# Differential attention in a two-layer hybrid encoder: the shift of the second softmax map per half, three of four transpose copies on ScalarE, all scaling on GpSimd

## The reference

```python
def block(args):                       # one block of 128 queries
    qb, bi = args
    qpos = bi * BLOCK + jnp.arange(BLOCK, dtype=jnp.int32)
    bias = table[:, t5_bucket(kpos[None, :] - qpos[:, None])]
    sc = jnp.einsum('bqhmd,bkhmd->bmhqk', qb, k).astype(jnp.float32) * scale + bias[None, None]
    p = jax.nn.softmax(sc, axis=-1)
    a = p[:, 0] - lam * p[:, 1]
    return jnp.einsum('bhqk,bkhd->bqhd', a.astype(v.dtype), v)
```

## Time and profile before

| | us |
|---|---|
| median of 3 runs | 4045.36 (4042.28 to 4050.85) |
| the profiled execution | 4044.97 |
| its span in the profile | 4043.2 |
| `diff_attention` of the first layer, first matmul to last output | 1184.88 to 1693.16 |

### The profile page before, as it was taken

One profiled execution on the slowest core, in us unless ns is written; L12 is line 12 of the kernel. 1 busy time (PEld: TensorE's weight loads), 2 busy tenths in 40 slices (PEclk: granted clock), 3 DMA queues, 4 the chain that ended last, 5 costly groups with the idle time before them and its releaser, 6 DMA issues. The chain is left out here.

```text
span 4043.2 us, 51539 instructions
## 1 busy us (share of the span) xinstructions
PE 3793.2 (94%) x19002; PEld 2624.1 (65%) x19002; DVE 2236.1 (55%) x3973; ACT 1658.7 (41%) x2886; POOL 2286.1 (57%) x1381
## 2 busy tenths in 40 slices
PE   8999999999989999889989999999999899998898
PEld 8789774555546666557777897755555466665577
DVE  3003125555569999875531030255556699998755
ACT  3102103333348888760031021033333488887610
POOL 1221325877768888744512213267777688886455
PEclk9999999999999999999989999999999999999999
DMA  5433445233420222245354334422233202223353
GB/s 176 126 132 118 145 134 123 62 82 71 91 59 1 57 57 58 57 112 190 130 174 130 128 120 140 144 68 55 66 73 77 59 1 57 57 58 72 109 177 135
DMA packets 180864, 392.43 MB, mean 97 GB/s; under 512 B 18014, under 2 KB 100168, under 8 KB 168968
## 3 DMA queue, kind: packets, MB, share of 16 engines
q1 hardware_dynamic: 179752, 387.75, 34.3%
q10 hardware_dynamic: 864, 1.41, 0.2%
HBM read 255.93 MB, written 135.67 MB: 97 GB/s over the span
## 5 line engine op out<-in xcount | busy, mean ns | idle before, releaser
L1297 POOL TENSOR_TENSOR mla_sum_pool<-mla_sum_pool,mla_probs 128x1024 f32<-128x1024 f32 (+1 forms) x336 | 777.8, 2315 | 209.0 <-ACT mla_probs L1258 184.2
L1315 DVE TENSOR_REDUCE carry_row_max<-psum 128x1 f32<-128x512 f32 x688 | 474.2, 689 | 416.1 <-PE psum L1130 411.2
L1258 ACT ACTIVATE mla_probs<-psum 128x1024 f32<-128x1024 f32 x384 | 373.3, 1021 | 694.4 <-PE psum L1167 689.7
L1690 DVE TENSOR_REDUCE diff_row_max<-psum 128x1 f32<-128x1024 f32 x512 | 613.4, 1217 | 49.6 <-PE psum L1534 38.9
L1613 ACT ACTIVATE diff_probs<-psum,diff_shift 128x1024 f32<-128x1024 f32 x512 | 566.1, 1111 | 178.0 <-DVE diff_shift L1697 171.8
L1560 PE MATMUL psum<-ident,diff_probs 128*128 128x128 f32 x2048 | 328.1, 284 | 93.0 <-DVE diff_turned L1724 80.9
L638 PE MATMUL psum<-in_x_hi,in_w_hi 128*128 128x512 f32 x1024 | 409.4, 400 | 2.7 <-ACT in_mla_val L745 2.7
L638 PE MATMUL psum<-in_x_hi,in_w_lo 128*128 128x512 f32 x1024 | 405.5, 396 | 0.0
L638 PE MATMUL psum<-carry_firsts,in_w_hi 128*128 128x512 f32 x1024 | 404.5, 395 | 0.0
L1560 PEld LDWEIGHTS psum<-ident,diff_probs 128*128 128x128 f32 x2048 | 215.9, 141 | 265.0 <-issue 254.3
L1671 POOL TENSOR_TENSOR diff_probs<-diff_probs 128x1024 f32<-128x1024 f32 x128 | 305.8, 2389 | 141.6 <-ACT diff_probs L1621 141.3
(11 more groups left out here) (213 smaller groups left out, 7363.7 us busy)
## 6 DMA issues: line engine op xcount, KB each, us to landing
in_w_raw<-in_w_in SPq DMA_DIRECT2D x64, 512.0 KB, 3.9
split_d<-in_out SPq DMA_DIRECT2D x64, 512.0 KB, 2.7
raw_d<-in_out SPq DMA_DIRECT2D x32, 512.0 KB, 2.7
mq_d<-in_out SPq DMA_DIRECT2D x48, 256.0 KB, 3.6
mk_d<-in_out SPq DMA_DIRECT2D x48, 256.0 KB, 4.0
carry_firsts<-split_d SPq DMA_DIRECT2D x48, 256.0 KB, 8.1
carry_weights<-split_d SPq DMA_DIRECT2D x48, 256.0 KB, 7.7
carry_weights<-split_d SPq DMA_DIRECT2D x16, 768.0 KB, 18.1
```

The costliest lines, as they stand in the source:

```text
L1258: nc.scalar.activation(probs[:, s % RING, :].rearrange("p (a n) -> p a n", n=CH), psum[:, S0 + 2 * (s % 2):S0 + 2 * (s % 2) + 2, :], ACT.E ...
L1297: nc.gpsimd.tensor_tensor(acc, start, probs[:, s % RING, mine], ALU.add).then_inc(pool_added, 1)
L1315: nc.vector.tensor_reduce(row_max[:, u % 2, qb, n:n + 1], psum[:, sweep_bank(g), :], AX.X, ALU.max).then_inc(maxed, 1)
L1690: nc.vector.tensor_reduce(row_max[:, n % 2, m, half:half + 1], banks(n, m, half), AX.XY, ALU.max).then_inc(maxed, 1)
```

## The change

1. Scores come scaled. The queries of the differential heads are multiplied by 1/sqrt(32) as the input projection copies them out of PSUM (ACT's copy gets a scale, DVE's subtraction becomes a multiply and subtract), and the bias constants are no longer divided by it. The exponentials lose their scale.
2. Map 1 gets a shift for each half, `part_shift`, written by the maximum itself (a negated reduction). `exp` of a half of map 1 waits for that half's maximum alone. `to_shift` still makes the common shift of the map; ACT computes two correction factors `part` = exp(shift - part_shift) a unit, and DVE multiplies the two sums of map 1 by them before it adds up (the new instruction with semaphore `weighed`).
3. POOL does all scaling: two multiplications of 1024 columns, each by ratio and by the half's `part`; ACT's `scale` is gone.
4. ACT takes the transpose batches 0, 1 and 2, DVE takes batch 3. The lists of PE, ACT and DVE are reordered, so that there is one batch of transposes between two pieces of scores.

```diff
-            return (act_copied if c % 2 else dve_copied), 2 * n + c // 2 + 1
+            return (act_copied, 3 * n + c + 1) if c < 3 else (dve_copied, n + 1)
...
                         scores(n, 0, 0)
-                    turns(n - LAG - 1, 3)
+                    turns(n - LAG - 1, 1)
                     if on:
                         scores(n, 0, 1)
                     products(n, 0)
+                    turns(n - LAG - 1, 2)
+                    if on:
+                        scores(n, 1, 0)
+                    turns(n - LAG - 1, 3)
+                    products(n, 1)
                     turns(n - LAG, 0)
                     if on:
-                        scores(n, 1, 0)
-                    turns(n - LAG, 1)
-                    if on:
                         scores(n, 1, 1)
-                    products(n, 1)
-                    turns(n - LAG, 2)
...
+                def parts(n):
+                    act.wait_ge(shifted, 2 * n + 2)
+                    nc.scalar.activation(part[:, n % DEEP1, :], part_shift[:, n % 2, :], ACT.Exp,
+                                         bias=shift[:, n % 2, 1:2], scale=-1.0).then_inc(parted, 1)
...
                     if on:
-                        exp(n, 0)
-                    if n == UNITS:
-                        scale(n - 1)
-                    copy(n - LAG, 1)
-                    if 1 <= n < UNITS:
-                        scale(n - 1)
+                        exp(n, 0, 0)
+                        exp(n, 0, 1)
                     if n % 2:
                         odd_half((n - 5) // 2)
+                    copy(n - LAG, 0)
                     if on:
-                        exp(n, 1)
+                        exp(n, 1, 0)
+                    copy(n - LAG, 1)
+                    if on:
+                        exp(n, 1, 1)
+                        parts(n)
+                    copy(n - LAG, 2)
...
+                    for k, half in enumerate((0, 1) if n < LATE else (1,)):
+                        at = slice(half * HALF, (half + 1) * HALF)
+                        second = probs1[:, n % DEEP1, at]
+                        nc.gpsimd.tensor_scalar(second, second, ratio[:, n % 2:n % 2 + 1],
+                                                part[:, n % DEEP1, half:half + 1], ALU.mult, ALU.mult
+                                                ).then_inc(times_ratio, 1)
+                        pool.wait_ge(times_ratio, done + k + 1)
+                        nc.gpsimd.tensor_tensor(probs[:, n % DEEP, at], probs[:, n % DEEP, at], second, ALU.add
+                                                ).then_inc(mixed, 1)
...
                     dve.wait_ge(exped, 4 * (n + 1))
+                    dve.wait_ge(parted, n + 1)
+                    nc.vector.tensor_tensor(row_sum[:, n % 2, 1, :], row_sum[:, n % 2, 1, :], part[:, n % DEEP1, :],
+                                            ALU.mult).then_inc(weighed, 1)
+                    dve.wait_ge(weighed, n + 1)
                     nc.vector.tensor_reduce(totals[:, :, qb, h], row_sum[:, n % 2, :, :], AX.X, ALU.add
                                             ).then_inc(summed, 1)
...
                 for n in range(UNITS + DRAIN + 2):
                     on = n < UNITS
-                    copy(n - LAG - 1, 2)
                     if on:
                         maximum(n, 0, 0)
                         maximum(n, 0, 1)
                         to_shift(n, 0)
                     if n == UNITS:
                         mix(n - 2)
-                        ratios(n - 1)
-                        copy(n - LAG, 0)
+                    ratios(n - 1)
+                    if n == UNITS:
                         mix(n - 1)
-                    else:
-                        copy(n - LAG, 0)
-                        ratios(n - 1)
+                    copy(n - LAG - 1, 3)
                     if on:
                         maximum(n, 1, 0)
+                    if n % 2:
+                        output((n - 5) // 2)
+                    if on:
                         maximum(n, 1, 1)
                         to_shift(n, 1)
```

More of the change, by code:

```diff
@@ L369, in tile_banks, with tile_scale @@
             return psum[:, tile_slot(g):tile_slot(g) + 2, :].rearrange("p a n -> p (a n)")
+        def tile_scale(t):
+            return DIFF_SCALE if T_DQ <= t < T_DK else 1.0
         def use_freed(u):
@@ L833, in _ @@
                         else:
-                            nc.scalar.activation(out[:, s, :].bitcast(F32R), tile_banks(g), ACT.Copy).then_inc(tile_out, 1)
+                            nc.scalar.activation(out[:, s, :].bitcast(F32R), tile_banks(g), ACT.Copy, scale=tile_scale(t)
+                                                 ).then_inc(tile_out, 1)
             @block.vector
@@ L1428, in diff_attention @@
         dots = sb("dots", [P, 4])
-        row_max = sb("row_max", [P, 2, 2, 2])
+        row_max = sb("row_max", [P, 2, 2])
+        part_shift = sb("part_shift", [P, 2, 2])
         shift = sb("shift", [P, 2, 2])
+        part = sb("part", [P, DEEP1, 2])
+        late = sb("late", [P, UNITS - LATE])
         row_sum = sb("row_sum", [P, 2, 2, 2])
@@ L1602, in _, with exp @@
             def _(act):
-                def exp(n, m):
-                    act.wait_ge(shifted, 2 * n + m + 1)
-                    if m == 0 and n >= DEEP:
-                        act.wait_ge(turn_done, 4 * (n - DEEP + 1))
-                    if m == 1 and n >= DEEP1:
-                        act.wait_ge(mixed, 2 * (n - DEEP1 + 1))
+                def exp(n, m, half):
+                    if m == 0:
+                        act.wait_ge(shifted, 2 * n + 1)
+                        bias = shift[:, n % 2, 0:1]
+                        if n >= DEEP:
+                            act.wait_ge(turn_done, 4 * (n - DEEP + 1))
+                    else:
+                        act.wait_ge(maxed, 4 * n + 2 + half + 1)
+                        bias = part_shift[:, n % 2, half:half + 1]
+                        if n >= DEEP1:
+                            act.wait_ge(mixed, 2 * (n - DEEP1 + 1))
@@ L1609, in exp @@
                     dst = probs[:, n % DEEP, :] if m == 0 else probs1[:, n % DEEP1, :]
-                    if m == 0 and n >= 2:
+                    if n >= 2:
                         act.wait_ge(summed, n - 1)
-                    for half in range(2):
-                        nc.scalar.activation(dst[:, half * HALF:(half + 1) * HALF].rearrange("p (a n) -> p a n", n=CH),
-                                             banks(n, m, half), ACT.Exp, bias=shift[:, n % 2, m:m + 1], scale=DIFF_SCALE,
-                                             accum_out=row_sum[:, n % 2, m, half:half + 1]).then_inc(exped, 1)
@@ L1617, in scale @@
-                def scale(n):
-                    act.wait_ge(ratio_ready, n + 1)
-                    at = 0 if n < LATE else HALF
-                    first = probs1[:, n % DEEP1, at:at + CH]
-                    nc.scalar.activation(first, first, ACT.Copy, scale=ratio[:, n % 2:n % 2 + 1]).then_inc(act_scaled, 1)
+                    nc.scalar.activation(dst[:, half * HALF:(half + 1) * HALF].rearrange("p (a n) -> p a n", n=CH),
+                                         banks(n, m, half), ACT.Exp, bias=bias,
+                                         accum_out=row_sum[:, n % 2, m, half:half + 1]).then_inc(exped, 1)
@@ L1730, in mix @@
                     dve.wait_ge(ratio_ready, n + 1)
+                    factor = late[:, n - LATE:n - LATE + 1]
+                    nc.vector.tensor_scalar(factor, part[:, n % DEEP1, 0:1], ratio[:, n % 2:n % 2 + 1], None, ALU.mult
+                                            ).then_inc(late_ready, 1)
+                    dve.wait_ge(late_ready, n - LATE + 1)
                     nc.vector.scalar_tensor_tensor(probs[:, n % DEEP, 0:HALF], probs1[:, n % DEEP1, 0:HALF],
-                                                   ratio[:, n % 2:n % 2 + 1], probs[:, n % DEEP, 0:HALF],
+                                                   factor, probs[:, n % DEEP, 0:HALF],
                                                    ALU.mult, ALU.add).then_inc(dve_mixed, 1)
@@ L2468, in constants @@
     kb, qb = np.arange(NB)[:, None], np.arange(NB)[None, :]
-    far = f32(1.0 / DIFF_SCALE)
-    left, right = (kb <= qb - 2) * far, (kb >= qb + 2) * far
+    left, right = kb <= qb - 2, kb >= qb + 2
     lo_rows = (np.arange(2 * NB) >= NB).astype(f32)
```

56 lines of the change are left out of this document (27 added, 29 removed).

## The result

| | before | with the change |
|---|---|---|
| median, us | 4047.28 (4042.28 to 4050.85, 4 runs) | 4081.89 (4078.99 to 4083.55, 4 runs) |
| span of the profiled execution | 4043.2 | 4081.4 |
| ratio of the medians | | 1.0086, interval 1.0068 to 1.0103 |

The changed kernel is slower by 0.9%; 4,085 was forecast. As a difference, 40.6 us were forecast; the two profiled spans differ by 38.2 and the medians by 34.6, since one more run of the kernel before has moved its median from 4045.36 to 4047.28.

What follows compares the result with a forecast made beforehand. It took the single transpose bank and DVE's copy as the bound before (7.746 us a unit), a POOL and DVE ring after (8.07): 20.1 us a layer, +40.6 on 4044.97, so 4,085 us, range 4,060 to 4,104.

Steps and rivals of the forecast that it cites:

- The held instruction: DVE's new two-input multiplication of the sums waits for POOL's second addition to end: 0.8 to 1.8 us for 0.15.
- Rival 1: DVE's small multiplication of the sums is not held by POOL; 3,990 us, faster; chance 0.11.
- The pace: Distance from ratio to ratio, set by POOL and DVE: 8.07 us a unit, for 7.746 before.
- the second pointer operand of POOL's multiplication: POOL multiplying by ratio and part instead of ratio and a constant: 0.06 us each, bounds 0 and 0.08.
- Uniform over all units: The 8.07 us between ratios holds in every unit, whatever the query block.
- The ring: Ratio, POOL's multiplications and additions, held DVE instruction, next ratio: 7.95 us, 8.07 with the second pointers.
- The drain: After the last ratio of a layer, changed copies and POOL widths balance: 0, bounded by 2 us either way.
- Changes 1, 2 and 4 on other engines: Scaled scores cost zero; the new shifts, copies and order leave PE, DVE and ACT at 7.3 us a unit or less.
- PE's longer waits: Sign in the new trace: PE waits for more than before, spread over several places; no size given.
- The forecast for a kernel without the hold: Without DVE waiting for POOL, PE's ring and POOL's work set about 7.3 us a unit: 3,990 us.
- The ring of PE: PE's transposes, scores, bands and products with waits for copies: 7.27 us with the band in half 1, 6.82 in half 0.
- Rival 3: POOL's multiplication with two factors costs up to an addition's 2.37 us: pace 10.4, 4,375 us; chance 0.03.

Runs made afterwards that it cites:

- e1: Changed kernel with DVE's two-input multiplication of map 1's sums replaced by two one-input multiplications by pointer; 4012.60 us, ratio 0.9923 to the kernel before.
- e10: Changed kernel with DVE making one factor per half, no two-input multiplication of the sums, POOL multiplying by one pointer and 1.0; 4011.88 us, ratio 0.9921.
- e11: e10 with DVE's copy of transpose batch 3 put ahead of its last mixing in the drain; 4008.13 us, ratio 0.9912 to the kernel before.
- e8: e1 with POOL's second pointer replaced by 1.0, the halves' correction left out of the mixing; 4009.06 us in one run.
- e6: Changed kernel with DVE making one factor per half and POOL multiplying by one pointer with no second operation; 4389.74 us.

## Why the prediction was right, and where its steps were not

**The held instruction: right, in mechanism, place and size.** Forecast was 0.8 to 1.8 us, ending with POOL's second addition; it shows 1.25 and ends within 0.02 us of it. The Trainium skill (SBUF — State Buffer, on who interferes with whom), read literally, said so: what starts first keeps the ports for its whole length. The traces agree for both kinds of POOL instruction of 1024 columns, and e1 shows that a pointer form is free of it (204 ns beside a busy POOL). Rival 1 is out.

For very small POOL instructions the page's rule and the traces differ, and the measurement decides. Behind the earlier trace rows stand 32 such overlaps, not one: each of the 32 multiplications starts 0.07 to 0.15 us after a POOL power (operation `pow`) of 128 x 2, with 0.55 to 0.63 us of it left, and takes its usual 0.19 us. An instruction of 1024 columns beside a POOL power of a single column isn't held either, with 0.51 us left (it takes 1.28 us, as the late mixing does when it is not held; these rows are from the kernel before):

```profile
2022.08 0.55 POOL L2320 TENSOR_TENSOR out_rstd<-out_moments,out_half_neg 128x1 f32<-128x1 f32 x1 [4.81 <-DVE out_moments L2391]
2022.12 1.28 DVE L2404 SCALAR_TENSOR_TENSOR early_w_raw<-early_w_raw,out_moments,out_g_row 128x1024 f32<-128x1024 f32 x1
```

Whether the few elements, the operation or the time since its start frees the way wasn't tried and stays open.

**The pace: 8.12 for 8.07.** The step that was mis-sized is the second pointer operand of POOL's multiplication, taken as 0.06 us: 1.195 - 1.118 = 0.077. The estimate from the Trainium skill's figure (GPSIMD Engine Reference, section 7), 102 cycles for a small read command, had been 0.085 and the pace 8.12; the pace agrees to the second digit, the pointer is nearly right.

**"Uniform over all units": wrong.** I tested whether the held instruction falls into POOL's second addition by the sum of DVE's list from ratio to instruction, at most 6.2 to 6.6, against POOL's start at 5.15. But after ratio 0 DVE is there after 5.21 us (1195.10 to 1200.31), with no copy in its list yet, and POOL, one pointer dearer in each multiplication, starts its second addition after 5.28 (1200.38). The instruction came 0.07 us ahead of it, and as long as DVE kept a lead POOL alone set the pace: 2 x (1.28 + 2.36) = 7.28. The ring has two modes; which it is in depends on a lead of a few tenths, which I took from the steady list instead of following it from unit 0. Against 8.07 throughout, the eight fast distances give 8.0 us less (one of 5.79, seven that sum to 50.75), the long one 1.6 more and 53 at 8.12 another 2.6 more: 16.5 us a layer instead of 20.1.

**The drain, put at 0 with 2 us either way: +2.9 a layer.** PE waits for a copy that stands behind DVE's last mixing:

```profile
1698.21 2.09 DVE L1759 SCALAR_TENSOR_TENSOR diff_probs<-diff_probs,diff_late 128x1024 f32<-128x1024 f32 x1
1700.22 0.68 DVE L1748 COPY diff_turned<-psum 128x512 f32<-128x512 f32 x1
```

```profile
1701.04 1.07 PE L1574 MATMUL psum<-ident,diff_probs 128*128 128x128 f32 x8 [1.81 <-DVE diff_turned L1748]
```

The mixing has two inputs in SBUF itself and is held by POOL. Before, the two mixings took 2.14 and 1.27 us, now 1.28 and 2.09, and it is the second for which PE waits in the end: it starts at 1698.21 under a POOL multiplication of 1.20 us from 1698.03. Whoever starts second is held, POOL too. Before, and in e10, DVE's last mixing starts first, and POOL's addition takes 3.33 us for 2.36, its multiplication 2.21 for 1.12:

```profile
1682.77 1.27 DVE L1731 SCALAR_TENSOR_TENSOR diff_probs<-diff_probs,diff_ratio 128x1024 f32<-128x1024 f32 x1
1682.93 3.33 POOL L1671 TENSOR_TENSOR diff_probs<-diff_probs 128x1024 f32<-128x1024 f32 x1
```

```profile
1657.41 1.28 DVE L1759 SCALAR_TENSOR_TENSOR diff_probs<-diff_probs,diff_factors 128x1024 f32<-128x1024 f32 x1
1657.47 2.21 POOL L1684 TENSOR_SCALAR diff_probs<-diff_probs,diff_factors 128x1024 f32<-128x1024 f32 x1 [2.66 <-DVE diff_factors L1740]
```

Moving the copy (e11 against e10) gives back 0.9 us a layer; the rest wasn't followed. The two misses, -3.6 and +2.9 a layer, nearly cancel: that the time was nearer than its parts is luck.

**Changes 1, 2 and 4 on other engines.** Change 1 costs nothing that shows: up to 1184 us PE is busy for 1142.01 us, 1141.78 before. The prediction's remark that the 94% of the earlier trace rows is mostly the input projection is a slip, since the page's share is over all stages; in the first 600 us alone PE is busy 97% (579.53 us), so that it is the bound there all the same. ACT's copies take 0.598 us (0.59 forecast). Of the signs named, PE's longer waits came (57 us in the windowed stretch for 45), but not spread over several places: 42 of them are for DVE's copy, as 39 were before. The forecast for a kernel without the hold was 7.3 us a unit and 3,990; e1 gives 7.40 and 4,012.6. 12 us of this come from the 0.10 (2 x 62 x 0.10), 8.5 from drains of 21.0 and 22.6 us in the two layers instead of 17.6. The ring of PE that I added up, 7.27 with the band in half 1, is 7.36 to 7.85 in the ratios: PE waits 0.29 to 0.31 us in several places there, for a copy of ACT or for a PSUM slot that ACT hasn't read yet (e1):

```profile
1404.60 0.73 PE L1542 MATMUL psum<-carry_weights 128*128 128x512 f32 x2 [0.29 <-ACT diff_probs L1631]
...
1408.06 0.63 PE L1574 MATMUL psum<-ident,diff_probs 128*128 128x128 f32 x4 [0.31 <-ACT diff_turned L1648]
```

I had left out the slot. That POOL's 7.28 isn't the bound of e1 is shown by e8 and e10; which chain is, between PE and ACT, was only read, not tried. Rival 3, a multiplication of POOL far dearer, is out for two factors. e6 has one that is, for another reason, its form; that its price (345 us over before) is close to the 330 given to the rival is chance.

## What to carry to other kernels

An instruction of two elements can take nearly as long as its longest neighbour (here 2.27 us beside 2.38), if it has two tensor inputs in SBUF on VectorE and GpSimd is full of instructions of 1024 columns: ahead of a value that GpSimd itself waits for, write it with pointer operands. When an instruction can fall on either side of a neighbour's start, follow the lead from the first unit on: one late arrival can lock the ring for the rest of the stage, and a faster neighbour can lock it sooner. And try the change without its one new hazard before judging it: here the plan was worth 0.8%, and the form of its smallest instruction cost 1.7%.

## What the runs showed of the hardware that was not expected

- A multiplication on GpSimd (128 x 1024) by one pointer takes 1.12 us if a second operation, a multiplication by 1.0, is written, and 2.84 us with none: the operation that does nothing saves 1.7 us. All 252 multiplications of e6 show it (2.83 to 2.88), and the median of e10's 252 does not (1.12). Why is not known.
- The hold also falls under a GpSimd instruction with a single tensor input (0.69 us at 1235.95), and on GpSimd itself where VectorE starts first (3.33 us for 2.36 at 1682.93 in the kernel before). The prediction's sum had looked at GpSimd's additions alone.
- The ratio of unit 0 lay between 1190.25 and 1197.27 us in these runs, though the stages ahead of it differ in nothing but the scale of the scores. The distances of e1 and e8 within the stage agree to 0.03 us in nearly all units, so a difference of 3 us in one whole run is better read inside the stage.
